# The end of a hybrid decoder block: two groups of the down projection kept in PSUM, and the last reads and row sums rearranged

## What is computed

```
x    = x + rms_norm(mix_out, norm_mix_post)                    # called x1 below
h    = rms_norm(x, norm_ffn_pre)
gate = causal_dwconv(h @ ffn_w_gate, ffn_conv_w, ffn_conv_b)   # 2048 -> 5632, width 3
up   = h @ ffn_w_up                                            # 2048 -> 5632
z    = (gelu(gate) * up) @ ffn_w_down                          # 5632 -> 2048
out  = x + rms_norm(z, norm_ffn_post)
```

## Time and profile before

| what | us |
|---|---|
| median of 3 runs (2946.89 to 2948.75) | 2947.95 |
| the profiled execution | 2945.31 |
| its span, first to last instruction | 2943.7 |
| PE busy in the span | 2824.3 (96%) |
| DVE busy | 1670.4 (57%) |
| ACT busy | 1198.8 (41%) |

### The profile page before, as it was taken

One profiled execution on the slowest core, in us unless ns is written; L12 is line 12 of the kernel. 1 busy time (PEld: TensorE's weight loads), 2 busy tenths in 40 slices (PEclk: granted clock), 3 DMA queues, 4 the chain that ended last, 5 costly groups with the idle time before them and its releaser, 6 DMA issues.

```text
span 2943.7 us, 37831 instructions
## 1 busy us (share of the span) xinstructions
PE 2824.3 (96%) x13823; PEld 2374.8 (81%) x13823; DVE 1670.4 (57%) x1865; ACT 1198.8 (41%) x1463; POOL 365.3 (12%) x433
## 2 busy tenths in 40 slices
PE   7999999999999999999969999999999999999996
PEld 6888888888888888888758888888888888888875
DVE  4232343344333234432688777777777777777757
ACT  3243443432222222222444545544555555554544
POOL 1000001000000000000001121221221221221223
PEclk9999999999999999999979999999999999999998
DMA  4233224332223334434424687788788787788786
GB/s 181 89 89 108 90 90 118 89 107 86 89 90 92 101 90 153 157 132 154 143 70 167 150 182 161 157 176 167 156 171 172 155 175 169 157 173 169 154 172 217
DMA packets 451765, 405.90 MB, mean 138 GB/s; under 512 B 13278, under 2 KB 357474, under 8 KB 448624
## 3 DMA queue, kind: packets, MB, share of 16 engines
q1 hardware_dynamic: 395552, 291.53, 31.9%
q0 software_dynamic: 51536, 105.05, 22.3%
q10 hardware_dynamic: 4608, 8.39, 0.7%
HBM read 300.06 MB, written 104.86 MB: 138 GB/s over the span
## 4 chain that ended last, share of the span: by engine, by line
PE 62%; DMA 13%; DVE 11%; issue 8%; ACT 5%; POOL 1%; ACTq 1%; DVEq 0%; SPq 0%; POOLq 0%
PE ps L552 18%; DMA down_sums<-arena 12%; PE ps L555 9%; PE ps L777 6%; PE ps L844 6%; PE ps L576 3%; PE ps L577 3%; PE ps L578 3%; PE ps L848 3%; DVE op_ring L1893 3%; ACT op_ring L1206 2%; PE ps L881 2%; DVE sum_ring L1879 2%; PE ps L882 2%; PE ps L883 2%
## 5 line engine op out<-in xcount | busy, mean ns | idle before, releaser
L1492 DVE TENSOR_TENSOR w_lo<-raw,w_hi 128x2048 fp32r<-128x2048 f32 x124 | 284.2, 2292 | 563.1 <-ACT w_hi L970 563.1
L1453 POOL DMA_DIRECT2D down_sums<-arena x320 | 277.1, 1093 | 982.1 <-ACT arena L1249 964.9
L1249 ACT COPY arena<-ps 128x512 f32<-128x512 f32 x336 | 179.6, 587 | 415.0 <-DMA down_sums<-arena 413.5
L970 ACT CAST w_hi<-raw 128x2048 fp32r<-128x2048 f32 x124 | 236.4, 1907 | 260.8 <-PE ps L578 205.1
L552 PE MATMUL ps<-h_hi,w_hi 128*128 128x512 f32 x1152 | 281.3, 397 | 1.1 <-ACT w_hi L970 1.1
L555 PE MATMUL ps<-h_hi,w_lo 128*128 128x512 f32 x1152 | 272.8, 389 | 0.0
L552 PE MATMUL ps<-h_lo,w_hi 128*128 128x512 f32 x1152 | 272.8, 389 | 0.0
L844 PE MATMUL ps<-hl,op_ring 128*128 128x512 f32 x1064 | 268.1, 394 | 3.3 <-ACT op_ring L1206 2.3
L552 PEld LDWEIGHTS ps<-h_hi,w_hi 128*128 128x128 f32 x1152 | 217.6, 191 | 48.2 <-ACT w_hi L970 1.5
L552 PEld LDWEIGHTS ps<-h_lo,w_hi 128*128 128x128 f32 x1152 | 216.3, 188 | 44.9
L555 PEld LDWEIGHTS ps<-h_hi,w_lo 128*128 128x128 f32 x1152 | 216.3, 188 | 44.9
(11 more groups left out here) (318 smaller groups left out, 4624.6 us busy)
## 6 DMA issues: line engine op xcount, KB each, us to landing
raw<-in_w_in SPq DMA_DIRECT2D x88, 1024.0 KB, 5.0
down_sums<-arena POOLq DMA_DIRECT2D x336, 256.0 KB, 6.4
quads<-in_ffn_w_gate SPq DMA_DIRECT2D x88, 512.0 KB, 4.7
quads<-in_ffn_w_up SPq DMA_DIRECT2D x88, 512.0 KB, 4.7
quads<-in_ffn_w_down SPq DMA_DIRECT2D x88, 512.0 KB, 5.5
raw<-in_w_out SPq DMA_DIRECT2D x20, 1024.0 KB, 5.0
merge_gates<-arena ACTq DMA_DIRECT2D x32, 256.0 KB, 2.0
raw<-in_w_up_a SPq DMA_DIRECT2D x8, 1024.0 KB, 5.2
```

The costliest lines, as they stand in the source:

```text
L970: act.copy(w_hi[:, s, :], raw[:, s, :]).then_inc(hi_ready, 1)
L1453: pool.dma_start(dst, src, accum_op=ALU.add).then_inc(acc_added[s], 16)
L1492: dve.tensor_tensor(w_lo[:, s, :], raw[:, s, :], f32(w_hi[:, s, :]), ALU.subtract).then_inc(lo_ready, 1)
```

## The change

It does four things, all in the last step and behind it.

- **Order** (`FINAL`): the four down operations of group 20 leave pair 2 and stand behind the last product, ahead of group 21. D3 of group 19 moves from behind M6 of pair 1 into pair 2, behind M2. The last four positions of the list become eight.
- **PSUM**: groups 20 and 21 are summed in the eight banks. For token tiles 0 and 1 all four parts of group 20 are computed first, then group 21 is added to the same banks; for tiles 2 and 3 both groups bank by bank, all parts of tile 2 first, then those of tile 3. Group 20 makes no stage copies and no adds to DRAM.
- **Buffers and reads**: the eight last down weights go to buffers 4 and 5 and to the quadrant buffers of the last pair, as these come free. Group 21's operands take four new slots in the buffers of h for M7 and M6. The sums are read back after M1 and M4 of the last pair; `z_gain` after M3, x1 of tiles 0 and 1 after M2, of tiles 2 and 3 after M5, with the down weights between them on the SP queue.
- **The last tiles**: a row tile is finished as soon as its own four parts are there. For tile 3 DVE makes all four column parts in three instructions (`last_rows`), and columns 1024 to 2047 get the norm weights on DVE (columns 1536 on into `z_last`, while ACT squares the same values).

The diff, cut to its core (of longer hunks only the new lines; "..." marks what is left out):

```diff
@@ -64,9 +64,11 @@
-FINAL = (woven(0) + woven(1) + [(2, q) for q in (M1, D0, M4, M3, D0 + 1, M2, M5, D0 + 2, M7, M6, D0 + 3)]
-         + [(3, q) for q in PRODUCTS] + [(4, D0 + d) for d in range(4)])
-PRODUCTS_END = len(FINAL) - 4
+FINAL = (woven(0) + [(1, q) for q in (M1, M4, M3, M2, D0 + 2, M5, M7, M6)]
+         + [(2, M1), (2, M4), (2, M3), (2, M2), (1, D0 + 3), (2, M5), (2, M7), (2, M6)] + [(3, q) for q in PRODUCTS]
+         + [(3, D0 + d) for d in range(4)] + [(4, D0 + d) for d in range(4)])
+PRODUCTS_END = len(FINAL) - 8
+TAIL_QUAD = {(3, 2): A22, (3, 3): A12, (4, 0): A11, (4, 1): A21}
@@ -229,7 +231,9 @@
+        op_hi, op_lo = ([op_ring[:, s, part, :] for s in range(3)] + [op_3[:, part * Q:(part + 1) * Q]]
+                        + [t[:, (2 * s + part) * Q:(2 * s + part + 1) * Q] for t in (h7, h6) for s in range(2)]
+                        for part in range(2))
@@ -243,9 +247,10 @@
-        x1_back = [h_rows[:, 8192:10240], h_rows[:, 10240:12288], h_rows[:, 0:2048], h_rows[:, 2048:4096]]
-        z_gain = h_rows[:, 12288:12288 + D]
-        z_junk = h_rows[:, 14336:14336 + 512]
+        x1_back = [h_rows[:, 0:2048], h_rows[:, 2048:4096], h_rows[:, 12288:14336], h_rows[:, 14336:16384]]
+        z_gain = h_rows[:, 8192:8192 + D]
+        z_junk = h_rows[:, 10240:10240 + 512]
+        z_last = h_rows[:, 10752:10752 + 512]
@@ -363,7 +368,9 @@
+            if sequence(i) is FIRST and pos < len(SLOT_FIRST):
+                return SLOT_FIRST[pos]
+            return pos % 4 + (4 if sequence(i) is FINAL and pos >= PRODUCTS_END + 4 else 0)
@@ -375,7 +382,9 @@
+            if slot_of(i, pos) > 3:
+                engine.wait_ge(ff_op, done(i, 3, M7 if slot_of(i, pos) < 6 else M6))
+            elif earlier:
@@ -389,7 +398,19 @@
+            part = tail_part(i, p, d)
+            if part is not None:
+                return ff_raw[part], 16 * (PAIRS * FF_STEPS + 1)
+            if isinstance(i, int) and i == LAST and p == 4:
+                return ff_raw[4 + d % 2], 16 * (2 * GROUPS - 2)
...
+        def tail_part(i, p, d):
+            return TAIL_QUAD.get((p, d)) if isinstance(i, int) and i == LAST else None
+        def down_quad(i, p, d):
+            part = tail_part(i, p, d)
+            return 4 + d % 2 if part is None else part
@@ -398,6 +419,8 @@
+        LAST_COLS = ((0, 1024), (1024, 1536), (1536, D))
+        TILE_BANKS = ((0, 2, 6, 4), (1, 3, 7, 5))
@@ -503,28 +530,46 @@
+                        if (p, D0 + d) in sequence(i) and (i, p) != (LAST, 3):
...
+            for d in range(2):
+                load_down(LAST, 3, d)
...
+                sp.wait_ge(acc_added[n], 16 * (2 if n == 0 else 1) * 4 * (GROUPS - 2))
...
+            sp.wait_ge(ff_sum, 5 * PAIRS * FF_STEPS - 1)
+            sp.wait_ge(ff_lo, done(LAST, 3, M4))
+            fetch_down(LAST, 3, 2)
+            fetch_down(LAST, 3, 3)
+            gone(M3)
+            sp.dma_start(z_gain, row_on_all(norm_ffn_post, 0, D)).then_inc(z_gain_loaded, 16)
+            sp.wait_ge(ff_sum, 5 * PAIRS * FF_STEPS)
+            sp.wait_ge(ff_lo, done(LAST, 3, M3))
+            fetch_down(LAST, 4, 0)
+            fetch_down(LAST, 4, 1)
+            gone(M2)
+            for n in HALVES[0]:
+                sp.dma_start(x1_back[n], x1_d[n, :, :]).then_inc(x1_loaded[0], 16)
+            for d in range(2):
+                sp.wait_ge(ff_lo, done(LAST, 3, D0 + d))
+                fetch_down(LAST, 4, 2 + d)
...
+            for n in HALVES[1]:
+                sp.dma_start(x1_back[n], x1_d[n, :, :]).then_inc(x1_loaded[1], 16)
...
+                for k, (a, b) in enumerate(((ZQ, ZM), (0, ZQ), (ZM, D)) if n < TT - 1 else LAST_COLS):
+                    if n < TT - 1 and k == 1:
+                        sp.wait_ge(fin_done_pool, n + 1)
+                    else:
+                        sp.wait_ge(fin_done_dve, 2 * n + (k + 1 if n == TT - 1 else k // 2 + 1))
@@ -921,37 +966,42 @@
+            def tail(d, n, bank, group, slot, first, last):
+                w = [t[slot].rearrange("p (j n) -> p j n", j=2) for t in (op_hi, op_lo)]
+                tok = slice(n * P, n * P + P)
+                for j in range(2):
+                    f = 2 * group + j
+                    pe.matmul(ps[:, bank, :], act_hi[:, f, tok], w[0][:, j, :], start=(first and j == 0), stop=False,
...
+                    pe.matmul(ps[:, bank, :], act_hi[:, f, tok], w[1][:, j, :], start=False, stop=False,
...
+                    mm = pe.matmul(ps[:, bank, :], act_lo[:, f, tok], w[0][:, j, :], start=False, stop=(last and j == 1),
...
+                if last:
+                    mm.then_inc(tail_done, 1)
+            pe.wait_ge(dn_evac, 16 * (GROUPS - 2))
+            pe.wait_ge(act_lo_ready, 2 * GROUPS - 2)
+            for d in range(4):
+                pe.wait_ge(ff_lo, done(LAST, 3, D0 + d))
+                if d == 2:
+                    pe.wait_ge(ff_part, 6 * (PAIRS * FF_STEPS - 1) + 4)
+                elif d == 3:
+                    pe.wait_ge(ff_part, 6 * PAIRS * FF_STEPS)
+                for n in HALVES[0]:
+                    tail(d, n, TILE_BANKS[n % 2][d], 0, d, True, False)
+            pe.wait_ge(act_lo_ready, 2 * GROUPS)
+            for d in range(4):
+                pe.wait_ge(ff_lo, done(LAST, 4, D0 + d))
+                for n in HALVES[0]:
+                    tail(d, n, TILE_BANKS[n % 2][d], 1, 4 + d, False, True)
+            for n in HALVES[1]:
+                for d in range(4):
+                    pe.wait_ge(down_evac, 2 * d + n % 2 + 1)
+                    tail(d, n, TILE_BANKS[n % 2][d], 0, d, True, False)
+                    tail(d, n, TILE_BANKS[n % 2][d], 1, 4 + d, False, True)
@@ -1256,7 +1306,7 @@
-                if k < len(ops) and ops[k][1] >= D0 and ops[k][0] < 4:
+                if k < (PRODUCTS_END if sequence(i) is FINAL else len(ops)) and ops[k][1] >= D0:
@@ -1317,30 +1367,39 @@
+            for d in range(4):
+                hi(LAST, PRODUCTS_END + 4 + d)
+            squares = [0]
+            def final_square(n, d):
+                count = squares[0]
+                squares[0] += 1
+                act.wait_ge(down_evac, count + 1)
+                if count:
+                    act.wait_ge(fin_squares, count)
+                act.activation(z_junk, acc[n][:, 512 * d:512 * d + 512], ACT.Square,
+                               accum_out=ss[:, 4 * n + d:4 * n + d + 1]).then_inc(fin_squares, 1)
...
+                act.wait_ge(fin_gain_pool, (6, 6, 9)[n])
...
+            for d in range(4):
+                for n in HALVES[0]:
+                    final_square(n, d)
+            final_square(2, 0)
+            final_scale(0)
+            final_square(2, 1)
+            final_scale(1)
+            final_square(2, 2)
+            final_square(2, 3)
+            final_square(3, 0)
...
+            for d in range(1, 4):
+                final_square(3, d)
@@ -1442,7 +1501,7 @@
-            for n_down in range(4 * (GROUPS - 1)):
+            for n_down in range(4 * (GROUPS - 2)):
@@ -1470,14 +1528,20 @@
+                for n in HALVES[0]:
+                    final_gain(n, d)
+            final_power(0)
+            final_power(1)
+            final_add(0)
+            final_gain(2, 0)
+            final_add(1)
+            final_gain(2, 1)
+            final_gain(2, 2)
+            final_power(2)
+            final_gain(3, 0)
+            final_add(2)
+            final_gain(3, 1)
+            final_power(3)
@@ -2079,54 +2143,81 @@
+            lo(LAST, PRODUCTS_END + 2)
+            after_m6(LAST, 3)
...
+            lo(LAST, PRODUCTS_END + 3)
...
+            for d in range(4):
+                lo(LAST, PRODUCTS_END + 4 + d)
+            tiles_done = [0]
+            def down_tile(n, d):
+                tiles_done[0] += 1
+                dve.wait_ge(tail_done, tiles_done[0])
+                dve.wait_ge(acc_back[n // 2], 32)
...
+                dve.tensor_tensor(part, part, ps[:, TILE_BANKS[n % 2][d], :], ALU.add).then_inc(down_evac, 1)
+            def gain_dve(n, d, to=None):
+                part = acc[n][:, 512 * d:512 * d + 512]
+                dve.tensor_tensor(part if to is None else to, part, z_gain[:, 512 * d:512 * d + 512], ALU.mult)\
+                    .then_inc(fin_gain_dve, 1)
...
+                dve.wait_ge(fin_squares, 6 + n + 1 if n < 2 else 4 * n + 4)
...
+                dve.wait_ge(fin_gain_dve, n + 1)
+                dve.wait_ge(fin_gain_pool, (6, 6, 9)[n])
...
+            def last_rows(n):
+                dve.wait_ge(fin_rstd_ready, n + 1)
+                dve.wait_ge(fin_gain_dve, 5)
+                dve.wait_ge(fin_gain_pool, 11)
+                for a, b in LAST_COLS:
+                    src = z_last if b == D else acc[n][:, a:b]
+                    dve.scalar_tensor_tensor(out=acc[n][:, a:b], in0=src, scalar=rstd[:, n:n + 1],
+                                             in1=x1_back[n][:, a:b], op0=ALU.mult, op1=ALU.add).then_inc(fin_done_dve, 1)
+            for d in range(4):
+                for n in HALVES[0]:
```

(61 more changed lines are left out.)

80 lines of the change are left out of this document (8 added, 72 removed).

## The result

The changed kernel takes 2918.84 us, median of 4 runs (2917.81 to 2923.37), beside 2948.35 of the kernel before on the same chip: a ratio of 0.9908, 95% interval 0.9895 to 0.9920, about 27 us faster (23.6 to 31; the two medians are 29.5 us apart). The prediction was 2920.8 us, a gain of 27.2.

A forecast was written before the change was run, and what follows sets the result against it. PE was taken to bound the kernel, losing 27.0 us to waits and low clock after 2812.6. Cutting that to 5.6 gains 21.4, the end 5.8, together 27.2: 2920.8 us predicted, range 2913 to 2932.

The forecast's parts named there:

- Matmuls, and PE's ideal: From 2812.6 us on, no matmuls added or removed; fourteen products and nine down operations still need 88.3 us of PE.
- Who made the gaps before: PE's 27.0 us loss: ACT waiting 32.4 us for adds with casts queued behind, and late norm weights making a 5.77 us gap.
- New loss on PE: In the changed order PE still loses 5.6 us: 3.5 waits, 1.6 low clock, 0.5 for a lo part.
- DVE is as full as PE: From M1 of pair 2 to M6 of pair 3, DVE has 44.0 us of work against PE's 44.5.
- it enters late: ACT waits 6.1 us for an add, so DVE starts the moved operations late; PE waits 3.5 us.
- DVE holds PE: Rival, chance 0.24: products back to back lose 14.2 us at the first step's rate; total 2929.4 us.
- Loads of the last pair: Weights for the last pair land before PE's turn at M1; no cost by itself.
- Group 20 behind the products: After the last product, 10.9 us of group 20 matmuls cover DVE and ACT finishing hidden tiles; that gap and slow clock go.
- The SP queue: Group 21's late down weights, at worst 14 us after the last product, cost nothing; without cover up to 6 us.
- The tail: Groups 20 and 21 together: 192 matmuls, 43.8 us without a gap if banks are free; the 5.77 us gap goes.
- Behind the last matmul: The end after PE's last matmul falls from 15.8 to 10.0 us, 5.8 less; bounds 9 and 13.
- The low clock stays: Rival, chance 0.04: the clock falls in the dense final matmuls and stays low, costing 38.4 us; total 2959.2 us.

The follow-up runs named there:

- The exchange on ACT: Changed kernel, with ACT making the cast (hi part) for operation k+3 before the fourth stage copy of operation k-1 in the last step; ratio 0.9870 to the kernel before.
- The exchange on ACT alone: Kernel before, with ACT's cast for operation k+3 put ahead of the fourth stage copy in its last step only; ratio 0.9981.
- hi_first_again: Second run of the changed kernel with ACT's cast ahead of the fourth stage copy in the last step; 2907.3 us, ratio 0.9872 to the kernel before.
- after_again: The changed kernel itself, run once more as the measure for other runs; 2919.4 us, ratio 0.9912 to the kernel before.
- the version with all steps: Changed kernel, with ACT's cast ahead of the fourth stage copy in every step of the channel mixer; 2864.62 us, ratio 0.9725 to the kernel before.

## Why the prediction was right, and which of its steps were not

**Matmuls, and PE's ideal.** Fourteen products and nine down operations in 88.3 us: right. The exchange on ACT reaches it within 0.1 us.

**Who made the gaps before.** The adds of group 20: 8.0 of the 13.3 us up to the last product, shown by leaving them out. The norm weights: the 5.77 us gap, shown by reading them early. Both as argued. The exchange on ACT alone, with all adds in place, takes 6.3 of the same 13.3: much of what the adds cost goes through the casts queued behind them.

**New loss on PE.** Predicted 5.6 us, measured 6.1. The size was right, but partly by luck, since the parts were not. The 1.6 us for a spell of low clock did not come; instead pair 3 has the same gaps again, 0.80 and 0.26, and 0.20 for a lo part, since D3 brings ACT the same wait for an add once more (5.54 us), where the layout had DVE in time from D3 on. And the step "DVE is as full as PE" named the wrong cause. Its count of 44.0 us is near DVE's 44.44 busy, but with the same work and the casts in time PE loses nothing. What the step "it enters late" said, a wait for an add ahead of a cast, was the whole of it. PE waited for banks, not, as laid out, for lo parts (3.5 of the 3.7 us of gaps up to M6 of pair 3).

**The rival "DVE holds PE"**, 14.2 us, took the first step's stretch as a rate. D3 behind M6 gives 0.9 us more, not 8.6, and that from a wait for weights.

**Loads of the last pair.** No cost, right: DVE waits 1.71 us for them and no gap of PE follows.

**Group 20 behind the products** covers the last hidden tiles: no gap behind M6, right.

**The SP queue.** Cost nothing, right; the third piece could be cast 11.0 us behind the last product, where the bound said 14 plus the cast's turn. With 2 MB more ahead it is 15.4. The Trainium skill's rule (DMA: Bandwidth & Descriptors, "Queues, rings and completion order") that each DMA engine takes the descriptors of a ring in order agrees with the 4.4 us.

**The tail**: no gaps from banks, right; 0.38 us once for the lo part of group 20's D3, where 0.5 was taken.

**Behind the last matmul.** Predicted 10.0 us with a lower bound of 9, measured 8.5, outside it. The mis-sized term is the row instruction: 3.95 us for 2048 columns by the rate of a row end beside POOL, 2.61 measured with POOL idle; the earlier trace rows has the 2.96 with POOL's addition beside it, and the rate was carried over to an end without one. The power took 0.55, not 1.0; the last store 3.4, not 2.9 (2913.8 to 2917.2).

**The low clock stays**: did not come; the granted clock is 1.00 from the parting to the last matmul.

**The sum.** 21.4 + 5.8 = 27.2 predicted, 20.9 + 7.3 = 28.2 from the mark on, 27 in time.

**The signs.** Three of the five for "right" came: 6.1 us lost on PE, no gap behind M6, the norm weights in time. Two did not: ACT's waits for adds are 11.3 us, not under 10, and the end is 8.5 us, not 9.5 to 10.5. Of those for "wrong", one came in small: the 0.20 us that a lo part holds PE in pair 3. It is gone with the exchange on ACT, so it did not stand for a full DVE.

What stays open: leaving out the adds of group 20 and the exchange on ACT were not run together on the kernel before; and of the 12 us by which the medians of `hi_first_again` and `after_again` differ, only some 6.7 lie behind the mark. The code ahead of it is the same, so the rest is put down to the runs, which is not shown.

## What to carry to other kernels

Where an engine works through a fixed order, look at what stands behind each of its waits, not only at how long it waits: a copy that waits for its buffer costs nothing by itself as long as the next operation that wants its bank is far off (where it was near, PE waited 3.55 us), while a cast queued behind it starves two engines. Gaps of one microsecond that look like a slightly late producer add up over a loop (25 us of 976 here, and more in time), and moving one call past another removed them all: that was worth more (43 us) than the whole change (27). And a last stage is shortened by bringing work that depends on nothing new to stand ahead of it, and by ending one row tile after the other.

## What the runs showed of the hardware

Not expected in this size: DVE's row ends, which read and write SBUF alone, are slowed while POOL works on its tiles of 512 columns. A row end of 1536 columns takes 2.95 to 3.42 us beside POOL and 1.94 with POOL nearly idle; 2048 columns take 2.61 us without. The additions that read a PSUM bank take 0.67 to 0.69 us either way. POOL's one-column power took 0.55 us with DVE idle and 0.93 beside a DVE instruction. A kernel that gives DVE's work to POOL to share it may get nothing for it, as the last tile shows.

The time at which the same instruction of the same code starts moves by up to 14 us of 2810 from one profile to the next, more than most single effects here. Distances between two instructions of one profile repeat better, within some 0.6 us for the changed order (105.7 and 106.3; 99.6, 99.5 and, for the version with all steps, 99.6) and within 1.4 for that of before (79.7 and 81.2 us from the mark to M6 of pair 3, with only the norm weights' read between them).
